# A three-slot tail for the key/value ring of the sampled attention, and fewer waits ahead of the merge weights

## The reference

```python
h = rmsnorm(x, g_pre_mix) * (1 + sc1) + sh1
qa, ka, va, qb, kb, vb, logf, ga, gb = mixer_inputs(h, w_in, b_f, pos)
oa, ob, state = attend(qa, ka, va, qb, kb, vb, logf)      # A: dilated windows, B: forgetting attention over 2048 past rows
mix = ((ga * (oa @ w_pa)) + (gb * (ob @ w_pb))) @ w_o     # merge_branches
x = x + gt1 * rmsnorm(mix, g_post_mix)
h2 = rmsnorm(x, g_pre_ffn) * (1 + sc2) + sh2
x = x + gt2 * rmsnorm(hier_moe(h2, ...), g_post_ffn)      # 32 experts, top 2 of one group of 8
```

## Time and profile before

| | us |
|---|---|
| time, median of 3 runs | 1101.23 |
| the three runs | 1101.21, 1101.23, 1106.16 |
| time of the profiled execution | 1101.23 |
| its span in the profile | 1099.0 |
| TensorE busy | 971.0 (88%) |
| VectorE busy | 384.0 (35%) |
| ScalarE busy | 206.5 (19%) |
| GpSimd busy | 186.9 (17%) |

### The profile page before, as it was taken

The page is one execution under the profiler, slowest core; times in us unless marked ns, Lnnn a source line. Parts: engine busy times, 40 slices in busy tenths (PEclk is TensorE's granted clock), DMA queues, the critical chain, the costliest instruction groups (busy, mean ns, idle before and its releaser), DMA issues.

```text
span 1099.0 us, 17873 instructions
## 1 busy us (share of the span) xinstructions
PE 971.0 (88%) x7308; PEld 568.1 (52%) x7308; DVE 384.0 (35%) x889; ACT 206.5 (19%) x505; POOL 186.9 (17%) x210
## 2 busy tenths in 40 slices
PE   5999999999889999899999899899879987777860
PEld 4444444444456656666667565445545544444430
DVE  4100033223877474763057413025511320000006
ACT  4000000001554211021100213122322211111114
POOL 0000033311220102222220211000023332122110
PEclk9999999999999899999999999899879999999995
DMA  9996766796877999999999888995689999999956
GB/s 294 384 365 250 256 245 235 258 323 200 281 258 261 325 323 374 350 366 333 370 329 344 310 303 299 386 345 243 248 301 372 367 384 387 386 385 392 410 217 258
DMA packets 101805, 349.32 MB, mean 318 GB/s; under 512 B 11642, under 2 KB 59650, under 8 KB 82782
## 3 DMA queue, kind: packets, MB, share of 16 engines
q1 hardware_dynamic: 80414, 261.50, 66.1%
q0 software_dynamic: 15552, 79.97, 19.9%
q10 hardware_dynamic: 5760, 6.72, 2.0%
HBM read 336.31 MB, written 63.36 MB: 364 GB/s over the span
## 4 chain that ended last, share of the span: by engine, by line
PE 36%; DMA 20%; DVE 5%; issue 2%; ACT 2%; SPq 1%; ACTq 0%; DVEq 0%; POOLq 0%
DMA w_all<-in_w_exp 12%; PE bank L1668 7%; PE bank L2107 6%; PE bank L2276 5%; DMA bias<-c_past 3%; PE bank L2127 3%; PE bank L1606 3%; PE bank L1660 2%; DVE mods L1790 2%; PE bank L1544 2%; PE bank L1658 1%; DMA c_past<-w_all 1%; PE bank L2093 1%; PE bank L1529 1%; DMA turned<-in_w_o 1%
## 5 line engine op out<-in xcount | busy, mean ns | idle before, releaser
L1668 PE MATMUL bank<-turned,w_all 128*128 128x320 f32 (+1 forms) x512 | 143.3, 424 | 5.3 <-ACT w_all L1716 3.7
L485 PE MATMUL bank<-w_all,turned 128*128 128x481 f32 (+2 forms) x384 | 120.3, 503 | 1.4 <-DVE turned L736 1.3
L485 PE MATMUL bank<-w_ring,turned 128*128 128x481 f32 (+2 forms) x384 | 118.4, 502 | 0.0
L2107 PE MATMUL bank<-w_all,mix_row 128*64 128x256 f32 x736 | 93.5, 411 | 27.1 <-DMA w_all<-in_w_exp 25.9
L1668 PEld LDWEIGHTS bank<-turned,w_all 128*128 128x128 f32 x512 | 93.9, 193 | 39.9 <-issue 19.5
L2107 PEld LDWEIGHTS bank<-w_all,mix_row 128*64 128x64 f32 x736 | 61.7, 149 | 65.9 <-issue 46.2
L1790 DVE STREAM_TRANSPOSE mods<-w_all 128x2048 f32<-128x2048 f32 (+1 forms) x39 | 86.2, 2236 | 11.0 <-PEq L814 3.9
L485 PEld LDWEIGHTS bank<-w_ring,turned 128*128 128x128 f32 (+1 forms) x384 | 57.1, 171 | 60.4 <-issue 57.3
L485 PEld LDWEIGHTS bank<-w_all,turned 128*128 128x128 f32 (+1 forms) x384 | 56.5, 171 | 61.6 <-issue 58.3
L2153 DVE COPY act_t<-bank 128x128 f32<-128x128 f32 x33 | 9.6, 291 | 199.2 <-PE bank L2117 197.5
L746 DVE COPY w_all<-bank 128x481 f32 (+5 forms) x32 | 16.9, 531 | 152.0 <-PE bank L485 151.8
(11 more groups left out here) (357 smaller groups left out, 1259.8 us busy)
## 6 DMA issues: line engine op xcount, KB each, us to landing
w_all<-in_w_exp SPq DMA_DIRECT2D x22, 2048.0 KB, 39.9
out_a_sample<-in_cache_a SPq DMA_DIRECT2D x8, 4080.0 KB, 21.4
w_all<-in_w_exp SPq DMA_DIRECT2D x25, 1024.0 KB, 37.7
mods<-in_w_ada SPq DMA_DIRECT2D x18, 1024.0 KB, 7.4
w_all<-in_cache_a SPq DMA_DIRECT2D x22, 512.0 KB, 7.8
w_all<-in_cache_a SPq DMA_DIRECT2D x40, 256.0 KB, 5.8
turned<-in_w_exp SPq DMA_DIRECT2D x5, 2048.0 KB
mods<-in_w_exp SPq DMA_DIRECT2D x5, 2048.0 KB, 42.8
```

The lines of the kernel that those rows point to most:

```text
L485: mm = nc.tensor.matmul(m.banks[i][r:r + ROWS[i], 0:hi - lo], m.hT[:, k, i * P:i * P + ROWS[i]], ring[u][:, CW * k + lo:CW * k + hi], star ...
L1668: mm = nc.tensor.matmul(GATE[:, 0:WIDTH[h]], gate_w[b][k][:, c % 2 * P:(c % 2 + 1) * P], m.hT[:, k, 256 * h:256 * h + WIDTH[h]], start=k = ...
L2107: mm = nc.tensor.matmul(m.banks[2 + p][x * SLOTS:(x + 1) * SLOTS, 0:HID], hgT[:, k, :], m.weights(u)[:, (2 * k + x) * HID:(2 * k + x + 1) ...
```

## The change

Two things change in phase C.

First, the last 11 steps, 81 to 91, no longer take slot n mod 6 but go round three slots, 4, 5, 0. Step 81 takes slot 4, 82 slot 5, 83 slot 0, 84 slot 4, and so on; step n from 84 on takes the slot of step n-3. Slots 1, 2 and 3 are used last by steps 73, 74 and 75 for values and by 79 and 80 for keys.

Second, SP's waits ahead of `w_o` and `w_pa` follow from that: one wait for the last value use of slots 1, 2, 3 stands ahead of `w_o` in place of the one for slots 2 and 3, the wait for `v_used` of 40 (`v_num[N - 7] + 1`, step 85) stays as it is, and the second wait, ahead of `w_pa`, is gone. The order of SP's instructions is the same as before.

```diff
-    slot_of = [n % KV_RING for n in range(N)]
+    TAIL, TAIL_SLOTS = 11, (4, 5, 0)
+    slot_of = [n % KV_RING if n < N - TAIL else TAIL_SLOTS[(n - N + TAIL) % 3] for n in range(N)]
     before = [max((x for x in range(n) if slot_of[x] == slot_of[n]), default=None) for n in range(N)]
...
             sp.wait_ge(mixed, 2 * KD)
             sp.wait_ge(gate_pe, len(sums))
-            last_use = lambda r: max(v_num[n] for n in v_num if slot_of[n] == r) + 1
-            sp.wait_ge(v_used, max(last_use(2), last_use(3)))
+            sp.wait_ge(v_used, max(v_num[n] for n in v_num if slot_of[n] in (1, 2, 3)) + 1)
             sp.wait_ge(turned, len(k_num))
...
                 sp.dma_start(rest[:, :, cols], w_o[:, slots:KD, cols]).then_inc(m.wo_in[h], 16)
-            sp.wait_ge(v_used, max(last_use(1), last_use(2)))
             sp.dma_start(m.slot(0)[:, 0:2 * D], I["w_pa"]).then_inc(m.wp_in, 16)
```

## The result

The changed kernel took 1117.67 us (median of 4 runs, 1117.20 to 1118.02) against 1103.70 for the kernel before (4 runs, 1101.21 to 1108.78), a ratio of 1.0129 with a 95% interval of 1.0081 to 1.0178. It is slower, as forecast, but by 14.0 us where the forecast was 8.0, and the time lies 2.7 us above the upper end of the range. Of these 2.7 us, 2.5 are in the kernel before: the forecast was built on 1101.23, and its median is now 1103.70. Four more executions of the changed kernel, the profiled one among them, took between 1113.49 and 1126.07; the median of all eight is the same 1117.67. Timed twice more, the same code gave 1.0076 (1.0047 to 1.0106) and 1.0105 (1.0074 to 1.0135), so the three timings have a mean of 1.0103, or 11 us. The profiled execution took 1116.79 (span 1114.6).

What follows compares the result with a forecast made beforehand. It took the end of phase C to be bound by when SP issues `w_o`, DMA engines nearly always busy. Phase D's start +7.1 and low clock +0.9 gave +8.0 on 1101.2: 1109.2 us, range 1103.5 to 1115.

Steps and rivals of the forecast that it cites:

- what holds `w_o`: SP's queue before phase D: `w_o` waits behind step 91's window, which waits for step 88; issued 8.2 us later.
- Step 84's wait: TensorE in the tail: step 84's load is issued only after step 81 is used, a wait of 2.8 us.
- Rival 3: Tail of phase C: loads keep pace and stay hidden, time within 1 or 2 us; chance 0.08.
- rival 4: Start of phase D: `w_o` goes out after step 85, 5 us sooner; 1096.5 us or a little less; chance 0.05.
- TensorE's work behind the wait for step 84: TensorE, steps 84 and 85: 1.55 us for step 84, 1.9 for transposes and `out_rows`, 1.0 for step 85.
- The walk: Steps 84 to 91, load by load: last value batch used at 708.4 against 699.7, phase D starting 7.1 us later.
- The price of a landing: Window batches in the tail: 4.7 us from last issue to landing, bounds 3.3 and 6.3.
- the credit of 1 us on `w_o`'s landing: First half of `w_o`: less window data ahead, about 0.5 MB against 1.5 MB, makes its 10.3 us landing 1 us shorter.
- The 0.9 us added for the clock: TensorE's last batches, at the low clock after half-used time: step 91's last 2.1 us double, 0.9 us of it counted.
- the signs named ahead: Profile signs of being right, among them first `w_o` product at 710 to 713 and everything from 740 shifted by one amount.
- Rival 1: Tail: crowded load prices (3.15 issues, 6.3 landing) or low TensorE clock in gaps; +10 to +14 us; chance 0.25.
- Rival 2: Tail: quick turns, landing at 3.3 and issues at 1.85; +4 us, 1105.2; chance 0.17.

Runs made afterwards that it cites:

- late_w_o: The kernel before, six slots kept, with only `w_o` held back until step 91 has been used: ratio 1.0068 (1.0035 to 1.0101).
- wait_back: The changed kernel with SP's wait for the last value batch put back ahead of `w_pa`: ratio to the kernel before 1.0088 (1.0056 to 1.0120).
- after_again: The changed kernel, unedited, timed a second time beside the kernel before: ratio 1.0076 (1.0047 to 1.0106).
- after_third: The changed kernel, unedited, timed a third time beside the kernel before: ratio 1.0105 (1.0074 to 1.0135).
- before_again: The kernel before, unedited, timed against itself as a measure of noise: ratio 1.0011 (0.9990 to 1.0032).
- w_o_in_lull: The changed kernel with `w_o`'s loads moved ahead of step 85's window in SP's queue, without their wait for step 85: ratio to the kernel before 1.0173 (1.0130 to 1.0216).
- half_bytes_after: The changed kernel with the second half of the value windows of steps 85 to 90 not loaded, same DMA count: ratio to the kernel before 1.0091 (1.0061 to 1.0121).
- two_issues_after: The changed kernel loading each value window with two DMAs of 512 KB instead of four of 256 KB: ratio to the kernel before 1.0096 (1.0064 to 1.0129).
- late_step_84: The kernel before, six slots kept, with only step 84's load held until step 81 has been used: ratio 1.0053 (1.0029 to 1.0077).
- four_slots: The changed kernel with four slots in the tail instead of three, and the waits that follow: ratio to the kernel before 1.0067 (1.0033 to 1.0102).
- tail_of_seven: The changed kernel with the three-slot tail cut to steps 85 to 91, so step 84 loads early: ratio to the kernel before 1.0112 (1.0072 to 1.0153).

## Why the prediction was right about the sign and wrong about the size

**Right: what holds `w_o`.** The prediction said that SP's queue, with step 91's window in it, moves the condition for `w_o` from step 87 to step 88 plus four issues, that the freed slots buy nothing, that `w_o` goes out 8 us later (9.6 measured from step 81), and that the rest shifts by one amount. The SP rows above show step 88's end, the window, and `w_o` in that order; late_w_o shows that such a delay by itself gives a loss of this kind; wait_back shows that the removed wait ahead of `w_pa` is worth nothing that these runs can tell. Step 84's wait was 3.26 us (2.8 forecast), 3.13 and 3.34 in the other two profiles. Rival 3 (hidden) and rival 4 (gains) are out.

**Wrong: TensorE's work behind the wait for step 84 was priced at full speed.** The failed step is the price "one `weigh`: 1.0 us (L1591, 1.93 for 32), 1.55 for steps 81 to 84", with the transposes "which took 1.9 us from the end of step 84". Both were read from a tail without waits, and the low clock was allowed only "for its last batches". The walk and the profiles, in us from step 81 (the column "used" is the end of step 85, which frees the slot for step 88):

| | 84 | 85 | used | 86 | 87 | 88 | `w_o` out | 91 | product |
|---|---|---|---|---|---|---|---|---|---|
| walked | 7.4 | 10.9 | 11.9 | 11.9 | 15.8 | 18.7 | 22.6 | 27.1 | 31.9 |
| changed | 8.0 | 11.6 | 13.2 | 14.0 | 18.1 | 21.0 | 24.1 | 28.3 | 34.4 |
| after_again | 7.8 | 12.6 | 14.3 | 14.1 | 17.5 | 20.8 | 24.7 | 28.0 | 34.7 |
| after_third | 8.0 | 12.2 | 14.1 | 13.9 | 18.1 | 20.7 | 23.8 | 28.1 | 35.3 |

Step 84 starts 0.4 to 0.6 us late against the walk: POOL issues 0.3 us after the slot is free, and the batch takes 6.0 to 6.2 us instead of 5.8. From there to the end of step 85 the walk has 4.5 us, the profiles 5.2, 6.4 and 6.1. TensorE's timeline of after_again, and its granted clock in 684 to 688 (0.50, the lower of its two levels):

```profile
683.95 1.93 PE L1605 MATMUL bank<-w_all,prob_t 128*32 128x256 f32 x16 [3.13 <-DMA w_all<-in_cache_b_v,value_rows]
...
686.81 1.97 PE L1562 MATMUL bank<-ident,w_all 128*128 128x128 f32 x8
688.75 1.61 PE L1590 MATMUL bank<-mods,prob_t 128*32 128x256 f32 x16
```
```profile
684.00:688.00 4.00, 4.00 (x26) 1.92 (x27) 1.01 (x3) 0.04 (x1) 0.00 (x0) 0.50 1.03 342
```

The same transposes in the kernel before:

```profile
685.38 1.09 PE L1563 MATMUL bank<-ident,w_all 128*128 128x128 f32 x8
```

From the start of step 84 to the end of step 85 the granted clock was 0.67, 0.53 and 0.56 in the three profiles, and 1.00 before. SP issues step 88's window in the moment in which step 85 ends (694.86, 690.41 and 690.24), so this loss goes straight into step 88, on which step 91's window and `w_o` depend. Step 88 is 2.3, 2.1 and 2.0 us late against the walk. The end of step 85 is 1.3, 2.3 and 2.2 us late: over half of it in the first profile and all of it in the other two.

**The price of a landing** (4.7 us, taken because at most two batches are in flight) was too low in the first profile only. From the last issue of step 88's window to TensorE's start it took 5.8 us (702.59 - 696.77) there, which adds 1.1, but 4.6 (696.87 - 692.31) and 4.7 (696.82 - 692.15) in the other two. Over all windows that TensorE waited for, the first profile has 5.4 to 6.5 us, above the 6.3 of my bounds once; the others have 4.4 to 5.7, but for step 91's half-sized last window, 3.5. Why one execution differs so much from the next was not found.

**Issues and the credit of 1 us on `w_o`'s landing.** The last window took 1.8 us to issue instead of the 2.6 walked, which gives 0.8 back. In after_again that is used up, as step 88 itself ran at the low clock (1.94 us). So `w_o` is 1.5, 2.1 and 1.2 us late. The step "with about 1.5 MB of windows ahead of it; now about 0.5 MB is ahead" was to make its landing 9.3 instead of 10.3 us. It took 10.4 (716.03 - 705.67), 9.9 and 11.4 in the three profiles of the changed kernel, 10.3 and 9.9 in the two of the kernel before, and 9.4 in late_w_o with nothing ahead: the credit is not seen. In the first profile the terms are 1.5 + 1.1 = 2.6 us, the difference between the 9.7 measured and the 7.1 walked for the start of phase D.

**The 0.9 us added for the clock** stood in the wrong place. Step 90 and what follows it did run slowly (1.94, 1.08 and 1.72 us), but ahead of a wait of 2.06 us for `w_o`, where it costs nothing, and the first products of phase D show only 0.2 more (8.18 against 8.01), as TensorE had waited there before as well. With all this put right the sum is 9.7 + 0.2 = +9.9 us, 1111.1: inside the range. The tail alone did not take the time out of it.

**The other 4 us** of the first timing, and the 2.5 us by which the base was low, are not in the tail. Two places where both kernels run the same code differ in the profiles: the start of step 81 lies between 673.7 and 683.2 in all kernels of the study, and the stretch from `w_o`'s first product to the end of the span between 395.0 and 400.2 (the two kernels with `w_o` split left out). The profiled execution of the changed kernel had 2.4 us more of the one and 3.5 more of the other (398.6 against 395.0, the lowest of all); before_again, with 398.0, shows that unchanged code does this by itself. So two of the signs named ahead failed: the first product came at 716.03 and not by 713, and the shift against the kernel before grew from 12.1 us there to 15.6 at the end of the span. The later timings, 1.0076 and 1.0105, put the cost at 8 and 12 us around the 9.7 to 10.8 of the profiles' tails. That the first timing fell on the high side is the reading that fits best, not a thing that a run proves. Why executions of one code differ by so much here was not found, so the larger part of the miss, 6.6 of 8.5 us, stays open.

**Rival 1** ("slow turns") had the right mechanism in its second condition, that TensorE falls to the low clock in the gaps. Its prices were too high: 13 us for `w_o`'s issue (9.4 to 10.3), an issue price of 3.15 (about 2), a landing of 6.3 (5.9 on average in the first profile, less in the others). That the first timing, +14.0, lies at the end of its +10 to +14 is luck, as 4 us of it are not in the tail. **Rival 2** (landing at 3.3, +4 us, a ratio of 1.0036) is refuted by the landings and by all three timings. Its 3.3 was one DMA: each window has four, and in the batch issued from 680.8 in the kernel before the first landed in 3.3 us and the last in 5.5. The 1 MB batch of step 84 took 6.1 us (689.56 - 683.48) in a stretch in which the DMA engines were busy at a share of 0.70. The Trainium skill (DMA: Bandwidth & Descriptors, the anatomy of one DMA on the SWDGE path) would give 4.4, an estimate by its fixed part and its rate; where they differ the measurement decides. Of the loads on the path only this one goes that way; the windows are issued by SP.

Where the gain went that freed slots seem to promise: `w_o` may start sooner by its slots but stands behind a window that depends on the narrowed ring. Even pulled ahead (w_o_in_lull) it delays the loads of the tail, which now have no slack. The six-slot ring of before had its loads in flight early, at 327 GB/s where the change has 152. What is lost with it is the head start of each load more than the bytes: with 3 MB less to carry (half_bytes_after) 8.4 of the 9.7 us remained.

## What to carry to other kernels

Count slots by the time that a load takes from issue to landing: here it is 6 to 8 us with its issues, and a batch is used up in 1 to 1.5, so that three slots can't keep up, four lost 6 us, and six just did. A place freed early is worth something only to a load that is not behind a dependent one in its queue, and only if the DMA engines have room for it. When walking such a chain, price the matmuls that free a slot at TensorE's lower clock where they stand behind a new wait (here about 3 us of wait made the next 4.5 us of work 0.7 to 1.9 us longer), and look whether a later wait hides slow work before adding it. Take a landing from the last DMA of a batch, and take the base of a forecast from more than three runs where they spread by 5 us.

## What the runs showed of the hardware that I had not expected

- The landing of `w_o`'s first half hardly depends on the windows ahead of it: 9.4 us with none in flight, 9.9 to 11.4 behind the last small window of the changed kernel, 9.9 and 10.3 with about 1.5 MB ahead. The longest, 12.2, is in two_issues_after.
- The price of the same 1 MB indirect load varies: 6.0 to 6.2 us in the changed kernel, 5.5 to 6.0 before, 9.3 in late_step_84 and 9.9 beside `w_o` in w_o_in_lull.
- TensorE's clock fell at the wait for step 84: the granted clock from the start of step 84 to the end of step 85 is 1.00 before and 0.53 to 0.67 after, and 8 transposes took 1.97 us instead of 1.09. In four_slots and tail_of_seven a fold went from 1.96 to 3.01 and 3.60 us. TensorE: Matmul & The Clock Gate, Part 1, in the Trainium skill says that idleness brings the clock down; the rows agree in kind.
- One code on one core differs by about 1% between executions: 1098.1 to 1109.4 in the 23 runs of the kernel before that were timed beside the last kernels. A change worth under 5 us can't be told from it in four runs.
